# Reordering the gate/up matmuls of one contraction step in an expert-choice encoder block

## The chip, the cores and the metric

The kernel runs on one core of one Trainium2 chip. The metric is the device time of one execution in microseconds (us), taken as the median of several runs. A profile of one more execution gives the time of each instruction.

## The reference, cut to what matters

One encoder block is applied to a prompt of 1024 tokens and a sample of 512 tokens with shared weights: attention and Fourier mixing, a gated output projection, then a mixture of 16 experts, then a norm. All data are fp32. The change is inside the experts. An expert takes its 192 best tokens (128 of the prompt, 64 of the sample) of width 1024 and runs a gated two-layer network of inner width 2048 on them:

```python
def expert_choice(xn, w_router, w_eg, w_eu, w_ed):
    ...
    aff = jax.nn.softmax((xt @ w_router).astype(jnp.float32), axis=-1)
    gate, idx = lax.top_k(aff.T, C)
    xe = xt[idx]
    h = jax.nn.silu(jnp.einsum('ecd,edf->ecf', xe, w_eg)) * jnp.einsum('ecd,edf->ecf', xe, w_eu)
    ye = jnp.einsum('ecf,efd->ecd', h, w_ed) * gate[..., None].astype(xn.dtype)
    out = jnp.zeros((T, D), xn.dtype).at[idx.reshape(-1)].add(ye.reshape(-1, D))
```

## The kernel before, in words

Each fp32 operand of a large product is split into a high part (rounded to fp32r) and a low part (the rest, also fp32r), and a product is made of three: high by high, high by low and low by high. For the experts the weights are split into `wh` (ScalarE, L1477) and `wl` (VectorE, L1520), and the 192 gathered tokens into `xsplit`, where the high columns and the low columns of one contraction step `k` lie side by side, 2 x 192 = 384 columns (CAP is 192).

The program of each engine is written out by hand, and engines wait for each other through counters (semaphores). TensorE runs its instructions in the written order. Its program for the experts is a loop over 16 experts; each does `gate_up` and then `down`.

`gate_up` loops over 16 blocks `q` of 128 inner columns. A block makes two outputs, `part` 0 (gate) and `part` 1 (up), each in its own PSUM bank, `2 * (q % 2) + part`. For each part it runs through 8 contraction steps `k`. One step has two matmuls, each with a weight tile of its own of 128 x 128:

- L1432: `wh` tile, 384 moving columns, into columns 0 to 383 of the bank (high and low tokens).
- L1434: `wl` tile, 192 moving columns (high tokens), added onto columns 192 to 383 of the same bank.

So a block has 2 x 8 x 2 = 32 matmuls and as many weight loads. Before its first matmul TensorE waits until the block's weights are cut (`w_cut`) and until the sums of the block two earlier, which used the same banks, have been taken out (`gu_sum`). After the block's last matmul one counter, `w_used`, is raised. ScalarE waits for it, copies the low columns of both banks out (L1491), splits a later weight block (L1477), and takes the sigmoid (L1498); VectorE adds the two halves of both banks (L1536), cuts the low weights (L1520) and forms the product of gate and up (L1543, L1545).

`down` multiplies the split inner activations `hsplit` with the down weights in matmuls of 512 columns, five per contraction step (L1451 to L1456), and `turn_tokens` transposes the next expert's tokens in its midst (L1416, L1417). The SyncE queue loads the raw weights (L1125), and it waits on `w_cut`, not on TensorE's order inside a block.

Other products of TensorE that the prediction compares with are the input projection (L549 to L551, 256 columns, fp32r) and the router's logits (L1175, 16 columns).

Of the kernel before, what the change touches and what calls it, by code (L numbers as in the profile page):

```python
# [34 lines left out]
P = 128  # L35
D = 1024
KT = D // P
# [118 lines left out]
def encoder(nc, x, rel_bias, norm1_g, w_in, w_attn_br, w_four_br, w_gate, b_gate, w_out, norm2_g,  # L156
            w_router, w_eg, w_eu, w_ed, final_g, identity, one_hot, pos_prompt, pos_sample, chan, y):
    ctx = ExitStack()
    with ctx:
# [161 lines left out]
        with nc.Block() as block:  # L321
            @block.sync
            def _(sp):
                sp.dma_start(relb[0:BUCKETS, :], rel_bias).then_inc(h_loaded, 16)
                sp.dma_start(hot[:, :], one_hot).then_inc(h_loaded, 16)
                for s in range(4):
                    sp.dma_start(xin[:, s, :], x[s * P:(s + 1) * P, :]).then_inc(x_in_ld[s], 16)
                    if s == 0:
                        sp.dma_start(g1[:, :], norm1_g.partition_broadcast(P)).then_inc(c_loaded, 16)
                        sp.dma_start(ident[:, :], identity).then_inc(c_loaded, 16)  # L330
                sp.dma_start(bg[:, :], b_gate).then_inc(c_loaded, 16)
                sp.dma_start(wr[:, :, :], w_router[0].rearrange("(k p) e -> p k e", p=P)).then_inc(c_loaded, 16)
                for n in range(2):
                    load_in_block(sp, n)
                with sp.Fori(1, NT // 4) as i:
                    for s in range(4):
                        sp.wait_ge(n_xs, i * 4 + (s - 3))
                        sp.dma_start(xin[:, s, :], x[bass.ds(i * 4 * P + s * P, P), :]).then_inc(x_in_ld[s], 16)

                sp.wait_ge(t_sb, ROWS_T // 2)  # L340
                sp.wait_ge(t_sbD, ROWS_T // 2)
                sp.dma_start(toep, toep_sb[:, :, :]).then_inc(t_out, 16)
# [1016 lines left out]
        with nc.Block() as block:  # L1359
# [48 lines left out]
            @block.tensor  # L1408
            def _(pe):
                def turn_tokens(n):  # L1410

                    pe.wait_ge(x_in, (n + 1) * 32)
                    pe.wait_ge(gu_sum, n * FT + GU_PAIRS)
                    for k in range(KT):
                        at_col = (k % 2) * CAP
                        pe.transpose(ps[:, k // 2, at_col:at_col + CAPS[0]], xg[0][:, k * P:(k + 1) * P], ident[:, :])  # L1416
                        mm = pe.transpose(ps[:, k // 2, at_col + CAPS[0]:at_col + CAP], xg[1][:, k * P:(k + 1) * P],  # L1417
                                          ident[0:CAPS[1], 0:CAPS[1]])
                        if k % 4 == 3:
                            mm.then_inc(x_T, 1)  # L1420

                def gate_up(e):
                    pe.wait_ge(x_cut, (e + 1) * 2)
                    for q in range(FT):
                        pe.wait_ge(w_cut, e * SUBS + (q + 1))
                        pe.wait_ge(gu_sum, e * FT + (q + 1))
                        for part in range(2):
                            bank = 2 * (q % 2) + part
                            for k in range(KT):
                                tile = slice((8 * part + k) * P, (8 * part + k + 1) * P)  # L1430

                                pe.matmul(ps[:, bank, 0:2 * CAP], wh[:, q % AHEAD, tile],  # L1432
                                          xsplit[:, k, :, :].rearrange("p s t -> p (s t)"), start=k == 0, stop=False)
                                mm = pe.matmul(ps[:, bank, CAP:2 * CAP], wl[:, q % AHEAD, tile], xsplit[:, k, 0, :],  # L1434
                                               start=False, stop=k == KT - 1)
                        mm.then_inc(w_used, 1)

                def down(e, last):
                    for i in range(8):
                        q, c = FT + i, i // 4  # L1440
                        pe.wait_ge(w_cut, e * SUBS + (q + 1))
                        if i < 4:
                            pe.wait_ge(h_cut, e * 8 + 2 * (i + 1))
                        if i % 4 == 0:
                            pe.wait_ge(y_ev, e * 2 + (c + 1))
                        for kk in range(4):
                            k = 4 * (i % 4) + kk
                            cols = slice(kk * CH, (kk + 1) * CH)
                            first, end = k == 0, k == FT - 1
                            prompt, sample = ps[:, 4 + 2 * c, :], ps[:, 5 + 2 * c, :]  # L1450
                            pe.matmul(prompt, hsplit[:, k, H_LOW], wh[:, q % AHEAD, cols], start=first, stop=False)  # L1451
                            pe.matmul(prompt, hsplit[:, k, H_HIGH], wh[:, q % AHEAD, cols], start=False, stop=False)  # L1452
                            pe.matmul(prompt, hsplit[:, k, H_HIGH], wl[:, q % AHEAD, cols], start=False, stop=end)  # L1453

                            pe.matmul(sample, hsplit[:, k, H_SAMPLE], wh[:, q % AHEAD, cols], start=first, stop=False)  # L1455
                            mm = pe.matmul(sample, hsplit[:, k, H_SAMPLE], wl[:, q % AHEAD, cols], start=False, stop=end)  # L1456
                        mm.then_inc(w_used, 1)
                        if i == 1 and not last:
                            turn_tokens(e + 1)

                turn_tokens(0)
                with pe.Fori(0, E - 1) as e:
                    gate_up(e)
                    down(e, False)
                gate_up(E - 1)
                down(E - 1, True)

# [183 lines left out]
```

## Time and profile before

| what | value |
|---|---|
| median of 3 runs | 3463.94 us (3463.56 to 3468.08) |
| span of the profiled execution, first to last instruction | 3481.5 us |
| TensorE matmul busy | 3295.9 us, 95% of the span |
| TensorE weight load busy | 2868.7 us, 82% |
| VectorE busy | 1858.5 us, 53% |
| ScalarE busy | 1433.8 us, 41% |
| DMA | 543.03 MB, mean 156 GB/s |

The span is all that the profile gives of the profiled execution's own time; it is 17.6 us (0.5%) above the median of the runs without it. A matmul is recorded as two instructions: a weight load (PEld in the rows) and the matmul itself (PE). The matmuls overlap in their records, so a matmul's recorded duration is longer than the time it adds; what it adds is read from the distance of starts.

### The profile page before, as it was taken

Reading aid. Unit: us, or ns where it says so; the run is one execution under the profiler, and the core shown is the slowest. Engines: PE = TensorE matmul, PEld = TensorE weight load, DVE = VectorE, ACT = ScalarE, POOL = GpSimd, SP = SyncE. Lnnn points to the kernel's source line nnn. Section 1 sums busy time; section 2 is a strip of 40 time slices with the busy share of each in tenths; the row PEclk is TensorE's granted clock in tenths of the full one; section 3 lists DMA queues with packets and bytes.
Section 4 is the critical chain, followed back from the end, with each engine's and each line's share of the span. In section 5 each row is a group of like instructions: output and inputs, shape, how many; then the busy total and the mean of one; then the engine's idle time right before and its main releaser. Section 6 shows DMA issues by size and latency. Waiting matters only on the chain. (4 is left out here: it accounts for less than half of the span.)

```text
span 3481.5 us, 45734 instructions
## 1 busy us (share of the span) xinstructions
PE 3295.9 (95%) x17656; PEld 2868.7 (82%) x17656; DVE 1858.5 (53%) x2770; ACT 1433.8 (41%) x1969; POOL 122.3 (4%) x133
## 2 busy tenths in 40 slices
PE   6999999999999999985999999999999999999994
PEld 4978989896487786544999999999999999999993
DVE  4140221305334332276677777777776777777774
ACT  4030120312333321323555555655565555555553
POOL 0000000000000000000000000000000000000000
PEclk9969979699999999986999999999999999999997
DMA  4000000003132335223677767777677767776774
GB/s 161 25 32 25 14 18 25 31 13 109 44 98 87 95 121 175 91 79 130 227 235 239 241 220 245 235 239 231 238 244 234 241 229 237 234 242 222 246 227 160
DMA packets 456895, 543.03 MB, mean 156 GB/s; under 512 B 13131, under 2 KB 372811, under 8 KB 456684
## 3 DMA queue, kind: packets, MB, share of 16 engines
q1 hardware_dynamic: 449644, 516.71, 44.1%
q0 software_dynamic: 7168, 25.17, 3.2%
q8 instruction: 57, 0.93, 0.1%
q14 instruction: 26, 0.21, 0.0%
HBM read 502.37 MB, written 39.47 MB: 156 GB/s over the span
## 5 line engine op out<-in xcount | busy, mean ns | idle before, releaser
L1432 PE MATMUL ps<-xsplit,wh 128*128 128x384 f32 x4096 | 1168.9, 360 | 2.2 <-DVE xsplit L1527 2.2
L1434 PE MATMUL ps<-xsplit,wl 128*128 128x192 f32 x4096 | 1026.6, 251 | 0.0
L1520 DVE TENSOR_TENSOR wl<-raw,wh 128x2048 fp32r<-128x2048 f32 x384 | 876.7, 2283 | 116.4 <-ACT wh L1477 115.3
L1477 ACT ACTIVATE wh<-raw 128x2048 fp32r<-128x2048 f32 x384 | 734.1, 1912 | 349.1 <-PE ps L1456 323.2
L1434 PEld LDWEIGHTS ps<-xsplit,wl 128*128 128x128 f32 x4096 | 784.0, 191 | 0.6
L1432 PEld LDWEIGHTS ps<-xsplit,wh 128*128 128x128 f32 x4096 | 770.2, 188 | 3.0 <-issue 2.4
L1491 ACT ACTIVATE low<-ps 128x384 f32<-128x384 f32 x256 | 126.0, 492 | 435.4 <-PE ps L1434 435.4
L1536 DVE TENSOR_TENSOR gu<-ps,low 128x384 f32<-128x384 f32 x256 | 142.8, 558 | 221.1 <-ACT low L1491 220.0
L1049 DVE TENSOR_TENSOR glow<-graw,ghigh 128x1024 fp32r<-128x1024 f32 x72 | 88.1, 1225 | 235.7 <-ACT ghigh L1005 235.7
L549 PE MATMUL ps<-whigh,xhigh 128*128 128x256 f32 x624 | 203.7, 326 | 3.5 <-ACT u L683 2.8
L550 PE MATMUL ps<-wlow,xhigh 128*128 128x256 f32 x624 | 203.6, 326 | 0.0
L551 PE MATMUL ps<-whigh,xlow 128*128 128x256 f32 x624 | 203.5, 326 | 0.0
L1451 PE MATMUL ps<-wh,hsplit 128*128 128x512 f32 x512 | 202.5, 395 | 0.0
L1453 PE MATMUL ps<-wl,hsplit 128*128 128x512 f32 x512 | 200.6, 392 | 0.0
L1455 PE MATMUL ps<-wh,hsplit 128*128 128x512 f32 x512 | 200.6, 392 | 0.0
L1456 PE MATMUL ps<-wl,hsplit 128*128 128x512 f32 x512 | 200.4, 391 | 0.0
L1452 PE MATMUL ps<-wh,hsplit 128*128 128x512 f32 x512 | 200.4, 391 | 0.0
L654 ACT ACTIVATE sc<-sc,negm 128x128 f32<-128x128 f32 (+2 forms) x144 | 61.9, 430 | 278.2 <-DVE negm L702 278.1
L1005 ACT ACTIVATE ghigh<-graw 128x1024 fp32r<-128x1024 f32 x72 | 76.3, 1060 | 213.9 <-DMA graw<-in_w_gate_dram 138.4
L990 PE MATMUL ps<-xh,ghigh 128*128 128x512 f32 x384 | 151.8, 395 | 13.1 <-DVE xlow L1056 13.1
L549 PEld LDWEIGHTS ps<-whigh,xhigh 128*128 128x128 f32 x624 | 153.6, 246 | 3.9 <-ACT u L683 3.0
L550 PEld LDWEIGHTS ps<-wlow,xhigh 128*128 128x128 f32 x624 | 153.6, 246 | 0.0
(205 smaller groups left out, 4626.7 us busy)
## 6 DMA issues: line engine op xcount, KB each, us to landing
raw<-in_w_exp_gate_dram SPq DMA_DIRECT2D x128, 1024.0 KB, 5.6
raw<-in_w_exp_up_dram SPq DMA_DIRECT2D x128, 1024.0 KB, 7.8
raw<-in_w_exp_down_dram SPq DMA_DIRECT2D x128, 1024.0 KB, 6.9
graw<-in_w_gate_dram SPq DMA_DIRECT2D x96, 256.0 KB, 2.9
wraw<-in_w_in_dram SPq DMA_DIRECT2D x12, 1024.0 KB, 5.0
graw<-in_w_four_br_dram SPq DMA_DIRECT2D x24, 384.0 KB, 3.5
xin<-in_x_dram SPq DMA_DIRECT2D x12, 512.0 KB, 3.9
xres<-in_x_dram SPq DMA_DIRECT2D x12, 512.0 KB, 3.6
```

The source lines that it names most:

```text
L549: pe.matmul(bank, high[k], whigh[:, n % 2, k, :], start=k == 0, stop=False)
L550: pe.matmul(bank, high[k], wlow[:, n % 2, k, :], start=False, stop=False)
L551: mm = pe.matmul(bank, low[k], whigh[:, n % 2, k, :], start=False, stop=k == KT - 1)
L1432: pe.matmul(ps[:, bank, 0:2 * CAP], wh[:, q % AHEAD, tile], xsplit[:, k, :, :].rearrange("p s t -> p (s t)"), start=k == 0, stop=False)
L1434: mm = pe.matmul(ps[:, bank, CAP:2 * CAP], wl[:, q % AHEAD, tile], xsplit[:, k, 0, :], start=False, stop=k == KT - 1)
L1451: pe.matmul(prompt, hsplit[:, k, H_LOW], wh[:, q % AHEAD, cols], start=first, stop=False)
L1452: pe.matmul(prompt, hsplit[:, k, H_HIGH], wh[:, q % AHEAD, cols], start=False, stop=False)
L1453: pe.matmul(prompt, hsplit[:, k, H_HIGH], wl[:, q % AHEAD, cols], start=False, stop=end)
L1455: pe.matmul(sample, hsplit[:, k, H_SAMPLE], wh[:, q % AHEAD, cols], start=first, stop=False)
L1456: mm = pe.matmul(sample, hsplit[:, k, H_SAMPLE], wl[:, q % AHEAD, cols], start=False, stop=end)
L1477: act.activation(cut_part(wh, q), raw_part(q), ACT.Copy).then_inc(w_high, 1)
L1520: dve.tensor_tensor(cut_part(wl, q), raw_part(q), cut_part(wh, q).bitcast(F32), ALU.subtract).then_inc(w_cut, 1)
```

## The change

Inside a block the loops over part and contraction step are exchanged, and within a step the two 384-column matmuls (gate, up) come first and then the two 192-column ones (gate, up). The number of matmuls, their operands, their banks, the order of the additions into each bank, the waits and the one counter raised at the block's end are the same.

```diff
                         pe.wait_ge(w_cut, e * SUBS + (q + 1))
                         pe.wait_ge(gu_sum, e * FT + (q + 1))
-                        for part in range(2):
-                            bank = 2 * (q % 2) + part
-                            for k in range(KT):
-                                tile = slice((8 * part + k) * P, (8 * part + k + 1) * P)
-
+                        for k in range(KT):
+                            gate_up_tiles = [(2 * (q % 2) + part, slice((8 * part + k) * P, (8 * part + k + 1) * P)) for part in range(2)]
+                            for bank, tile in gate_up_tiles:
                                 pe.matmul(ps[:, bank, 0:2 * CAP], wh[:, q % AHEAD, tile],
                                           xsplit[:, k, :, :].rearrange("p s t -> p (s t)"), start=k == 0, stop=False)
+                            for bank, tile in gate_up_tiles:
                                 mm = pe.matmul(ps[:, bank, CAP:2 * CAP], wl[:, q % AHEAD, tile], xsplit[:, k, 0, :],
                                                start=False, stop=k == KT - 1)
                         mm.then_inc(w_used, 1)
```

## Rows read from the trace of the kernel before

**Rows 1.** The profile's page: the span, and each engine's busy time.
```profile
span 3481.5 us, 45734 instructions
...
PE 3295.9 (95%) x17656; PEld 2868.7 (82%) x17656; DVE 1858.5 (53%) x2770; ACT 1433.8 (41%) x1969; POOL 122.3 (4%) x133
```

**Rows 2.** The page's costliest groups: the two gate/up matmuls (count, busy, mean).
```profile
L1432 PE MATMUL ps<-xsplit,wh 128*128 128x384 f32 x4096 | 1168.9, 360 | 2.2 <-DVE xsplit L1527 2.2
L1434 PE MATMUL ps<-xsplit,wl 128*128 128x192 f32 x4096 | 1026.6, 251 | 0.0
```

**Rows 3.** Busy time by stretch: one expert's `gate_up`, columns as its first line says.
```profile
core 0: us, PE busy (x) PEld busy (x) DVE busy (x) ACT busy (x) POOL busy (x), PEclk, DMA share, GB/s
2075.10:2148.00 72.90, 72.90 (x514) 72.86 (x513) 56.30 (x77) 46.15 (x56) 7.95 (x8) 1.00 0.72 239
```

**Rows 4.** TensorE's waits over the expert stage, 1619 to 3440 us, all of them.
```profile
PE ps L1432 <- DVE xsplit L1527: 2.2, 1, 2.2
```

**Rows 5.** Timeline, start of that `gate_up`: start us, us, engine, line.
```profile
2074.91 0.39 PE L1456 MATMUL ps<-wl,hsplit 128*128 128x512 f32 x1
2074.91 0.19 PEld L1432 LDWEIGHTS ps<-xsplit,wh 128*128 128x128 f32 x1
2075.13 0.33 PE L1432 MATMUL ps<-xsplit,wh 128*128 128x384 f32 x1
2075.14 0.19 PEld L1434 LDWEIGHTS ps<-xsplit,wl 128*128 128x128 f32 x1
2075.30 0.25 PE L1434 MATMUL ps<-xsplit,wl 128*128 128x192 f32 x1
2075.31 0.19 PEld L1432 LDWEIGHTS ps<-xsplit,wh 128*128 128x128 f32 x1
...
2075.39 0.36 PE L1432 MATMUL ps<-xsplit,wh 128*128 128x384 f32 x1
2075.41 0.19 PEld L1434 LDWEIGHTS ps<-xsplit,wl 128*128 128x128 f32 x1
```

**Rows 6.** Groups by line within 2075 to 2188 us: the expert's long gate/up matmuls.
```profile
L1432 PE MATMUL ps<-xsplit,wh 128*128 128x384 f32 x256 | 72.9, 359 | 0.0
```

**Rows 7.** Timeline, end of that `gate_up`: its last matmul and the next.
```profile
2147.84 0.25 PE L1434 MATMUL ps<-xsplit,wl 128*128 128x192 f32 x1
2147.92 0.41 PE L1451 MATMUL ps<-wh,hsplit 128*128 128x512 f32 x1
```

**Rows 8.** Timeline, the reading of one block's banks by ScalarE and VectorE.
```profile
2007.92 0.49 ACT L1491 ACTIVATE low<-ps 128x384 f32<-128x384 f32 x1 [1.60 <-PE ps L1434]
...
2008.44 0.56 DVE L1536 TENSOR_TENSOR gu<-ps,low 128x384 f32<-128x384 f32 x1 [0.60 <-ACT low L1491]
```

**Rows 9.** Timeline, input projection, 256 columns: first and last of 314 matmuls.
```profile
683.41 0.28 PE L550 MATMUL ps<-wlow,xhigh 128*128 128x256 f32 x1
...
720.97 0.28 PE L551 MATMUL ps<-whigh,xlow 128*128 128x256 f32 x1
```

**Rows 10.** Timeline, down product, 512 columns: first, three inner, last of 25.
```profile
2038.49 0.39 PE L1451 MATMUL ps<-wh,hsplit 128*128 128x512 f32 x1
...
2041.21 0.39 PE L1453 MATMUL ps<-wl,hsplit 128*128 128x512 f32 x1
2041.44 0.39 PE L1455 MATMUL ps<-wh,hsplit 128*128 128x512 f32 x1
2041.66 0.39 PE L1456 MATMUL ps<-wl,hsplit 128*128 128x512 f32 x1
...
2043.93 0.39 PE L1456 MATMUL ps<-wl,hsplit 128*128 128x512 f32 x1
```

**Rows 11.** Timeline, router's logits, 16 columns: sixteen weight loads in one row.
```profile
1549.75 1.87 PEld L1175 LDWEIGHTS ps<-wr,xn2T 128*128 128x128 f32 x16
```

**Rows 12.** Timeline, weight loads of the token transposes inside `down`.
```profile
2044.82 0.14 PEld L1417 LDWEIGHTS ps<-ident,xgS 64*128 64x128 f32 x1
2045.03 0.14 PEld L1416 LDWEIGHTS ps<-ident,xgP 128*128 128x128 f32 x1
2045.29 0.13 PEld L1417 LDWEIGHTS ps<-ident,xgS 64*128 64x128 f32 x1
```

## The prediction

> **What bounds the kernel now.** I read the page first: TensorE is busy for 95% of the span, the next engine for 53% [rows 1]. The two gate/up matmuls, 4096 of each, are its costliest groups [rows 2]. They lie in 16 experts; in the `gate_up` of one, 72.9 us long, TensorE is busy for all 72.90 us at a granted clock of 1.00, the higher of its two levels, while VectorE has 56.30 and ScalarE 46.15 [rows 3]. In the whole expert stage TensorE waits for another engine once, for 2.2 us [rows 4]. So the stage lasts as long as TensorE's own stream of loads and matmuls, and anything that this stream gains or loses is gained or lost by the kernel: 16 x 72.9 = 1166 us are at stake.
>
> **The cadence before.** The first short matmul of that expert starts at 2075.30 [rows 5], the last at 2147.84 [rows 7]; there are 256 [rows 6], thus 255 pairs in 72.54 us, 284.5 ns for a pair of one long (384) and one short (192) matmul. What makes up this number decides the prediction.
>
> Streaming first. The 512-column matmuls come 24 intervals in 5.44 us, 226.7 ns apart [rows 10]; the 256-column ones 313 intervals in 37.56 us, 120.0 ns [rows 9]. That is 0.417 ns a column and 13.3 ns a matmul. By this line a long one would take 173.3 ns and a short one 93.3, together 266.6. The pair takes 17.9 ns more, 73 us over 4096 pairs, and the question is whether the new order gives any of that back.
>
> The weight loads say where it goes. A load starts with the start of the matmul ahead of it, not earlier: 2075.14 after the matmul at 2075.13, 2075.31 after 2075.30 [rows 5]. So one tile can wait while another is in use, and no more. Under a long matmul the load is done in time: a long one begun after a 512-column one has its short successor start 0.17 us later (2075.13 to 2075.30). Under a short one it isn't: the load begun at 2075.31 is followed by the next one only at 2075.41, 0.10 us later, although the 192 columns are through before that. The 16-column matmuls show the same limit alone: 16 loads in 1.87 us, and with 0.19 for the record of the last, as of the loads in [rows 5], 15 intervals of 112 ns [rows 11], whatever the matmul. With 173 for the long one and 112 for the short one the pair comes to 285, and 284.5 is measured. So a long matmul costs its streaming, a short one costs the load of whatever comes next, and neither lends the other its slack.
>
> **The change, part by part.** It removes and adds no instruction: a step of one `k` has two long and two short matmuls and four loads in both orders, and there are 16 x 16 x 8 = 2048 steps. No DMA is issued in the moved lines, and no wait stands between them. What changes is the neighbours:
>
> - Two long ones in a row: the second is a long matmul that begins with its weights ready. Its price is between the 0.17 us of [rows 5] and the 173.3 ns of the line; call it 172.
> - Long to short stays as it is.
> - Two short ones in a row: the second starts when its load is done, like a long one now, and then the next load begins. This case, one load-bound start after another, doesn't occur in the present gate/up. The nearest row is the 16-column chain with the same 128 x 128 tile, 112 ns. From below the smallest distance is a load's own pace, 0.10 to 0.11 us in [rows 5], say 107. From above it is 120: a 256-column matmul has a load of fp32r weights under it too and needs no longer [rows 9]. I take 112, the row nearest in kind, since nothing but loads binds there.
>
> Of the four intervals of a step, one long and one short keep the sum of today's pair, 284.5. The other two are the second long one and the second short one: 172 + 112 = 284 in place of 284.5. The difference is -0.5 ns x 2048 = -1 us. With the ends: (170 + 107 - 284.5) x 2048 = -15 us, and (173.3 + 120 - 284.5) x 2048 = +18 us.
>
> The Trainium skill, page "TensorE: Matmul & The Clock Gate", section "LDWEIGHTS (loading the stationary operand)", gives a weight load as its columns divided by 1.2 in ns, which is 106.7 for 128. The second short interval at that price would make the step 172 + 106.7 - 284.5 = -5.8 ns and the kernel 12 us faster, an estimate; the 16-column chain's 112 ns [rows 11] stands against it, so I leave it as the lower case. The same page, in "Step-by-step: what each phase is for", says that loads are pulled ahead of running matmuls within a 64-deep window. Were that more than one tile ahead, the pairs of today would run at the streaming sum of 266.6; they take 284.5.
>
> Edits costed at nothing: the gate bank is now complete only at the block's end instead of its middle. Nobody notices, because the one counter was raised at the end before as well: ScalarE reads both banks from 2007.92 for 0.49 us and VectorE adds them from 2008.44 for 0.56, done at 2009.00 [rows 8]. These banks are needed again one block after, 16 pairs or 4.55 us later, so some 3.5 us of cover remain; without it TensorE would wait about 1.1 us in each of 256 blocks, 280 us. The first matmul of a block carries the same two waits, so the weights' loads and cuts see the same dates.
>
> **The sum.** The profiled span is 3481.5 us [rows 1], 17.6 us above the median of the runs, and gives its intervals only as differences; -1 us put onto the median of 3463.9 gives 3463 us.
>
> **The rivals.**
>
> - *Turn-free loads*, faster: the second of two load-bound starts costs a bare load, 107 ns, and the second long one 170 to 172. Then the step is 5.5 to 7.5 ns shorter, 11 to 15 us: 3449 to 3453. For it speaks the 0.10 between two loads in [rows 5]; against it the 112 of [rows 11].
> - *The bank*, faster: today each short matmul adds onto columns that the long one just wrote in the same bank, and the 17.9 ns above the streaming sum are a wait for that. The new order puts another bank's matmul between, and the whole 73 us come back: 3391. Against it: in the 512-column chain the bank changes between L1453 and L1455 and not between L1455 and L1456, and the distances are 0.23 and 0.22 [rows 10]; and the loads explain the excess without it.
> - *The full turn*, slower: the second short one pays a matmul's 13.3 ns on top of the load, 120 ns. The step becomes 172 + 120 - 284.5 = 7.5 ns longer, 15 us, with 173.3 for the long one 18: 3479 to 3482. It decides from 115.9 ns on (284.5 - 172 + 3.4, as 3.4 x 2048 = 7 us). For it: all fp32r rows that stream carry these 13.3 ns; against it, 173 + 120 would have made today's pair 293. Farther out lie the transposes, whose loads come 0.21 and 0.26 us apart [rows 12]; 235 in place of 112 would cost 250 us, but they alternate tiles of 64 and 128 rows, which no gate/up tile does.
> - *Order without effect* is the forecast itself: four matmuls cost what they cost whatever their neighbours.
>
> **How the numbers follow.** A measurement of this kernel tells from no change what is above 0.2%, 6.9 us. I give the forecast 0.74, its own range 3457 to 3470; turn-free loads 0.10; the bank 0.03; the full turn 0.10, and something larger on that side, as in [rows 12], 0.03. So faster 0.13, same 0.74, slower 0.13. The range from 3451 to 3482 holds the forecast, the full turn and most of the turn-free case, and leaves out the bank and the large loss.
>
> **What would show it right or wrong.** One expert's `gate_up` should last 72.8 us again, with TensorE busy throughout. In it the starts after a matmul should read about 0.20 (long to long, as today's matmul that waits for its load is recorded early), 0.17 (long to short), 0.09 (short to short) and 0.11 (short to long), in sum 0.57. The loads should be 0.11 apart twice and 0.17 twice. A long-to-long or long-to-short distance near 0.17 together with short ones at 0.09 throughout would show the bank; a sum of 0.58 the full turn. TensorE waits other than the one of 2.2 us would mean that an engine behind it has become late. The prediction fails if a load can start before the matmul ahead of it does, or if two short matmuls of different banks are dearer than two loads.

## The result and the profile after

The changed kernel takes 3481.53 us (median of 4 runs, 3479.60 to 3482.79), the kernel before 3464.02 us: a ratio of 1.0046, 95% interval 1.0032 to 1.0060, so it is slower by about 16 us by that ratio and by 17.5 by the two medians. No change was forecast, and the time lies just inside the stated range, at its far end.

The page of the changed kernel, its span, TensorE's busy time and the two groups that answer to [rows 2]:

```profile
span 3479.3 us, 45734 instructions
...
PE 3293.9 (95%) x17656; PEld 2866.0 (82%) x17656; DVE 1857.2 (53%) x2770; ACT 1433.8 (41%) x1969; POOL 119.7 (3%) x133
...
L1430 PE MATMUL ps<-xsplit,wh 128*128 128x384 f32 x4096 | 1100.5, 350 | 2.2 <-DVE xsplit L1526 2.2
...
L1433 PE MATMUL ps<-xsplit,wl 128*128 128x192 f32 x4096 | 741.0, 262 | 0.0
```

Two things on this page mislead. The busy sums of the two groups fall by 68 and 286 us against [rows 2], because matmuls of one line now overlap each other in their records; the kernel isn't faster for it. And the span is 2.2 us shorter than that of [rows 1]: in that earlier execution the first expert's first gate/up matmul started only at 1619.0 us, here at 1603.2, because the clock was low for longer in the stages ahead (276 us against 236), which neither order of the gate/up matmuls touches. Over the twelve traces of this document that start moves by 0.4 us for each us at the lower clock ahead of it. The experts have to be compared with each other.

The start and the end of one expert's `gate_up`, as in [rows 5] and [rows 7] (matmuls of one line that follow each other are one row, the last column their count):

```profile
2061.67 0.39 PE L1455 MATMUL ps<-wl,hsplit 128*128 128x512 f32 x1
2061.90 0.51 PE L1430 MATMUL ps<-xsplit,wh 128*128 128x384 f32 x2
2062.25 0.36 PE L1433 MATMUL ps<-xsplit,wl 128*128 128x192 f32 x2
2062.45 0.53 PE L1430 MATMUL ps<-xsplit,wh 128*128 128x384 f32 x2
...
2135.06 0.36 PE L1433 MATMUL ps<-xsplit,wl 128*128 128x192 f32 x2
2135.26 0.42 PE L1450 MATMUL ps<-wh,hsplit 128*128 128x512 f32 x1
```

From the first long matmul to the first matmul of `down` it takes 73.36 us here, and 2147.92 - 2075.13 = 72.79 in [rows 5, 7]. The same is seen from expert to expert. The first long matmul of the next expert here, and of the expert before that of [rows 5] in the kernel before:

```profile
2175.35 0.33 PE L1430 MATMUL ps<-xsplit,wh 128*128 128x384 f32 x1
...
1962.23 0.33 PE L1432 MATMUL ps<-xsplit,wh 128*128 128x384 f32 x1
```

2175.35 - 2061.90 = 113.45 us in place of 2075.13 - 1962.23 = 112.90, and these two numbers come again wherever the clock doesn't fall, so 16 x 0.55 = 8.8 us. That is half of the loss.

The other half is the clock. The busy time by stretch around the token transposes of two experts of the changed kernel (the columns are those of [rows 3], the last but two the granted clock), and last of one expert of the kernel before:

```profile
2029.30:2033.00 3.70, 3.70 (x18) 2.10 (x16) 1.65 (x3) 2.67 (x3) 0.00 (x0) 1.00 1.08 382
2033.30:2036.60 3.30, 3.30 (x9) 2.61 (x8) 2.65 (x3) 0.61 (x2) 0.00 (x0) 0.50 0.26 92
...
2144.40:2148.10 3.70, 3.70 (x18) 2.13 (x16) 1.65 (x3) 2.67 (x3) 0.00 (x0) 1.00 1.08 381
2148.40:2151.70 3.30, 3.30 (x16) 2.73 (x15) 2.68 (x3) 0.59 (x2) 0.00 (x0) 1.00 0.25 88
...
2157.00:2160.70 3.70, 3.70 (x18) 2.05 (x16) 1.65 (x3) 2.67 (x3) 0.00 (x0) 1.00 1.08 382
2161.30:2164.60 3.30, 3.30 (x9) 2.63 (x8) 2.90 (x3) 0.37 (x1) 0.00 (x0) 0.50 0.18 63
```

In all three, TensorE runs the 16 transposes for 3.7 us at the higher level. Behind the first and the last stretch the clock falls to half, to the lower level, and 9 matmuls lie in the next 3.3 us instead of 16; behind the second one it doesn't. An expert with such a fall is 1.6 us longer (115.06 us to the next one). There are 15 such stretches in the expert stage, one for each expert that has a next one. The trace of the changed kernel has 7 falls there, behind every second or third stretch, that of before 3 (from 1707.3, 2161.2 and 2953.1 us on), and another trace with the distance of before has 2 (e1 below). With the 8.8 us of cadence, 4 to 5 more falls at 1.6 us make 15 to 17.

### The profile page after: what moved, and what is told of

Read it like the earlier page. It is cut to its first block and busy times, and to the rows that moved or that the text cites. A ratio compares the mean times of both kernels' runs of the same rounds, so it can differ in the third digit from the quotient of the medians.

```text
span 3479.3 us, 45734 instructions
## 1 busy us (share of the span) xinstructions
PE 3293.9 (95%) x17656; PEld 2866.0 (82%) x17656; DVE 1857.2 (53%) x2770; ACT 1433.8 (41%) x1969; POOL 119.7 (3%) x133
## 5 line engine op out<-in xcount | busy, mean ns | idle before, releaser
L1430 PE MATMUL ps<-xsplit,wh 128*128 128x384 f32 x4096 | 1100.5, 350 | 2.2 <-DVE xsplit L1526 2.2
L1433 PEld LDWEIGHTS ps<-xsplit,wl 128*128 128x128 f32 x4096 | 742.0, 188 | 0.0
L1433 PE MATMUL ps<-xsplit,wl 128*128 128x192 f32 x4096 | 741.0, 262 | 0.0
L1430 PEld LDWEIGHTS ps<-xsplit,wh 128*128 128x128 f32 x4096 | 622.1, 192 | 3.5 <-issue 2.4
```

What stands on the lines that cost most here:

```text
L1430: pe.matmul(ps[:, bank, 0:2 * CAP], wh[:, q % AHEAD, tile], xsplit[:, k, :, :].rearrange("p s t -> p (s t)"), start=k == 0, stop=False)
```

## The experiments

Each comparison below was run against the kernel before on the same chip. "Distance" is the time from one expert's first gate/up matmul to the next one's where the clock doesn't fall, read from the trace, and "falls" are the stretches of lower clock in the expert stage of the one profiled execution. All of them begin within 0.9 us of the start of an expert's last transpose.

| kernel | distance, us | falls | ratio to before (95%) |
|---|---|---|---|
| before | 112.90 | 3 | |
| changed | 113.45 | 7 | 1.0046 (1.0032 to 1.0060) |
| e1: loops exchanged, alternating | 112.90 | 2 | 0.9999 (0.9990 to 1.0009) |
| e2: groups of 2 in one bank | 113.45 | 7 | 1.0042 (1.0030 to 1.0054) |
| e3: groups of 16 | 113.25 | 5 | 1.0027 (1.0018 to 1.0037) |
| e9: groups of 4 | 113.87 | 10 | 1.0079 (1.0067 to 1.0092) |
| e4: before, 64 more matmuls | 122.02 | 8 | one run, 3620.2 us |
| e5: before, 3 more long matmuls | 113.41 | 5 | 1.0037 (1.0025 to 1.0050) |
| e6: changed, 16 more long matmuls | 116.25 | 3 | 1.0149 (1.0126 to 1.0171) |
| e7: before, transposes spread | 113.37 | 0 | 1.0011 (1.0002 to 1.0021) |
| e8: changed, transposes spread | 113.92 | 0 | 1.0035 (1.0023 to 1.0046) |
| e10: before, transposes in halves | 112.99 | 0 | 0.9989 (0.9980 to 0.9999) |

**One part alone: the loops (e1).**

```diff
+for k in range(KT):
+    for part in range(2):
+        bank, tile = 2 * (q % 2) + part, slice((8 * part + k) * P, (8 * part + k + 1) * P)
         pe.matmul(ps[:, bank, 0:2 * CAP], wh[...], ...)
         mm = pe.matmul(ps[:, bank, CAP:2 * CAP], wl[...], ...)
```

> The loops over part and k are exchanged as in the change, but long and short matmuls still alternate (gate long, gate short, up long, up short). Theory of the loads (what costs is a short matmul right behind a short one): nothing changes, 568.8 ns for four matmuls, 72.70 us for the gate_up of one expert, 112.90 us from expert to expert, 3464 us. Rival (the banks: what costs is that gate and up alternate within a step): 573 ns for four matmuls, 73.24 us for one gate_up as in the changed kernel, 3473 us or more.

Measured: the distance is that of before, 112.90, and the time is too. Exchanging the loops, and with them alternating the banks from pair to pair, costs nothing.

**The other part alone: the groups (e2).** Here long and short stand for the two matmul calls:

```diff
 for part in range(2):
     bank = 2 * (q % 2) + part
-    for k in range(KT):
-        long(k); short(k)
+    for pair in range(0, KT, 2):
+        long(pair); long(pair + 1); short(pair); short(pair + 1)
```

> The loops stay as before (one part, one bank at a time), but two contraction steps are grouped: long, long, short, short, all into one bank. Theory of the loads: the cadence of the changed kernel, 573 ns for four matmuls and 73.24 us for the gate_up of one expert, 3473 us by the cadence alone and about 3481 us if the granted clock falls as often as in the changed kernel. Rival (the banks): 72.70 us and 3464 us.

Measured: the changed kernel's numbers, with the loops and banks of before. Its `gate_up`, again from the first long matmul to the first of `down`:

```profile
2062.04 0.51 PE L1432 MATMUL ps<-xsplit,wh 128*128 128x384 f32 x2
...
2135.39 0.42 PE L1452 MATMUL ps<-wh,hsplit 128*128 128x512 f32 x1
```

73.35 us, as 73.36 in the changed kernel. With e1 this settles the first question: what costs is that two long and two short matmuls stand together, and not where they write.

**The prices by themselves (e4).** Sixty-four matmuls, whose results the first block overwrites, run ahead of each expert:

```diff
+if q == 0:
+    def probe(i, n, bank):
+        cols = xsplit[:, i % KT, :, :].rearrange("p s t -> p (s t)")[:, 0:n]
+        pe.matmul(ps[:, bank, 0:n], wh[:, 0, i % 16 * P:(i % 16 + 1) * P], cols, start=True, stop=True)
+    for i in range(16):
+        probe(i, 384, 0)
+    for i in range(16):
+        probe(i, 384, i % 2)
+    for i in range(16):
+        probe(i, 192, 0)
+    for i in range(16):
+        probe(i, 192, i % 2)
```

> Before the first block of each expert 64 more matmuls run whose results the first block overwrites: 16 long into one bank, 16 long into two banks by turns, 16 short into one bank, 16 short into two by turns, each with a weight tile of its own. Theory of the loads: 173 ns from long to long, 112 to 115 ns from short to short, no difference between one bank and two, about 9.2 us more for each expert and 3611 us in all. Rival (the banks): chains in one bank and in two differ by some 5 ns or more. Rival (the full turn): 120 ns from short to short.

One run, 3620.2 us. The timeline, in order: long ones into one bank, into two by turns (matmuls), short ones into one bank, into two (their loads):

```profile
2097.90 1.37 PE L1430 MATMUL ps<-xsplit,wh 128*128 128x384 f32 x7
...
2099.46 2.76 PE L1430 MATMUL ps<-xsplit,wh 128*128 128x384 f32 x15
...
2102.40 1.31 PEld L1430 LDWEIGHTS ps<-xsplit,wh 128*128 128x128 f32 x11
...
2104.07 1.42 PEld L1430 LDWEIGHTS ps<-xsplit,wh 128*128 128x128 f32 x12
```

A row's length less the record of its last instruction (0.33 and 0.19), divided by the intervals: 173 and 174 ns from long to long, 112 and 112 from short to short. Both prices are what the prediction worked with, one bank or two. The rival of the full turn (120 ns) falls. A change of bank has no price here; the probes add onto nothing, so they don't test a wait for sums just written. But the chain showed something else: the long ones follow the 512-column matmuls of the expert before, and the first distances between them, the same in each expert (medians of the starts in the trace), are 171, 175, 177, 185, 176 and 182 ns before they settle at 173. A long matmul's price depends on its place in the run. This trace also has 8 falls of the clock, at 122.02 us from expert to expert.

**Longer groups (e3, e9).** All 16 long matmuls of a block first, and then all 16 short ones; and the same in groups of four (the diff is that of e9, where long and short stand for the two matmul calls; e3 takes all 16 at once):

```diff
+all_tiles = [(k, bank of part, tile of part and k) for k in range(KT) for part in range(2)]
+for four in range(0, 2 * KT, 4):
+    for k, bank, tile in all_tiles[four:four + 4]: long
+    for k, bank, tile in all_tiles[four:four + 4]: short
```

> The suspected cost is doubled: within a block all 16 long matmuls come first, then all 16 short ones. Theory of the loads, charged to each short matmul that follows a short one (15 per block in place of 8, 4.5 ns each): 73.8 us for one gate_up, 3481 us by the cadence, and more where the granted clock falls more often. Rival (charged to each change from long to short or back, 1 per block in place of 8): 72.8 us for one gate_up and 3465 us.

Measured for e3: 0.35 us more per expert than before, less than with groups of two (0.55), and neither theory's number: a charge for each short one behind a short one would have given about 1.1, a charge for each passage 0.1. Both fall. The trace shows where it sits. The loads around the passage from short to long, those of 16 short matmuls, of the first two long ones behind the run, and of the next five (a load starts with the matmul ahead of it):

```profile
2001.07 1.93 PEld L1432 LDWEIGHTS ps<-xsplit,wl 128*128 128x128 f32 x16
...
2002.91 0.30 PEld L1429 LDWEIGHTS ps<-xsplit,wh 128*128 128x128 f32 x2
...
2003.21 0.89 PEld L1429 LDWEIGHTS ps<-xsplit,wh 128*128 128x128 f32 x5
```

The short ones' loads are 112 ns apart, as in the chain. From the second long one's load on, the starts in the trace are 180, 176, 182 and then 173 ns apart (medians), where the settled price is 173: a run of short ones is paid for by the first three long ones behind it. From this came a number for groups of four, which have four such passages in a block, and in each group only the fourth long matmul has settled:

> Groups of four: four long matmuls (two contraction steps, gate and up), then four short ones. Theory of the settling (the first three long matmuls behind a run of short ones take about 180, 176 and 181 ns and only later ones 173, a short one 112 and the first of a run 108): 1154 ns for eight matmuls against 1137 when they alternate, 73.74 us for the gate_up of one expert, more than with groups of two (73.24) and of sixteen (73.05). Rival (a fixed charge of 4.5 ns for each change from short to long beyond the alternation): 73.0 us.

Measured for e9: 0.97 us more per expert than before, the worst of all groups, with the predicted settling in its loads (medians 180, 176, 182, 173, then 108, 111, 112 and 112). Its `gate_up`:

```profile
2076.86 0.51 PE L1430 MATMUL ps<-xsplit,wh 128*128 128x384 f32 x2
...
2150.63 0.42 PE L1450 MATMUL ps<-wh,hsplit 128*128 128x512 f32 x1
```

73.77 us against 72.79 before. A cost that rises from groups of two to four and falls again to sixteen is what the settling says and what a fixed charge for a passage doesn't.

**The clock without the groups (e5).** The order of before, with three long matmuls more per expert:

```diff
+if q == 0:
+    for i in range(3):
+        pe.matmul(ps[:, 0, 0:2 * CAP], wh[:, 0, i % 16 * P:(i % 16 + 1) * P],
+                  xsplit[:, i % KT, :, :].rearrange("p s t -> p (s t)"), start=True, stop=True)
```

> The kernel before, in its own order, with three more long matmuls at the start of each expert whose results are overwritten: about 0.52 us more for each expert, so that experts follow each other at 113.42 us, as in the changed kernel (113.45), without any grouping. Theory of the distance (how often the granted clock falls behind the token transposes depends on the distance from expert to expert, not on the order of the matmuls): 7 falls in the expert stage in place of 2 or 3, 1.6 us each, and 8.3 us of cadence, in all some 16 us above the kernel before. Rival (the grouped matmuls themselves draw the falls): 2 or 3 falls, 8 us above the kernel before.

Measured: a ratio of 1.0037, 13 us, of which 16 x 0.51 = 8 us are the added matmuls; 5 falls in the profiled execution, which was the fastest of six (3472.3 us; the median is 3479.4 at a lower mean clock). None of its gate/up matmuls is grouped, and it still loses some 5 us more than it was given to do. That speaks for the distance, though one profile with 5 falls against an expected 7 leaves the count rough.

**The clock with the groups, at another distance (e6).** The same insertion, sixteen times, in the changed kernel:

> The changed kernel with sixteen more long matmuls at the start of each expert whose results are overwritten: 2.77 us more for each expert, 44 us in all, experts 116.23 us apart. Theory of the distance (the number of falls follows the distance from expert to expert, and not in proportion to it): clearly fewer falls than the 7 of the changed kernel, 2 or 3, and 3518 us. Rival (the falls belong to the grouped matmuls): 7 falls, 3526 us.

Measured: 3518.5 us (two runs), and 3 falls instead of 7. With the groups in place the falls grow rare at this distance. It isn't that more distance means fewer falls: e4, with the gate/up order of before, has 8 at 122.02 us. So the count goes by the distance, not in proportion to it, and not by the grouped matmuls.

**The clock without the stretch of transposes (e7, e8).** In both kernels a pair of transposes behind each five 512-column matmuls, over two blocks of the down product:

```diff
 mm = pe.matmul(sample, hsplit[:, k, H_SAMPLE], wl[...], ...)
+if i in (1, 2) and not last and (i, kk) != (1, 0):
+    turn_tokens(e + 1, [4 * (i - 1) + kk - 1])
...
-if i == 1 and not last:
-    turn_tokens(e + 1)
+if i == 2 and not last:
+    turn_tokens(e + 1, [KT - 1])
```

> The kernel before, with the eight pairs of token transposes no longer in one stretch inside the down product but one pair behind each five 512-column matmuls. Theory of the transposes (the clock falls because of the stretch of 3.7 us that holds only transposes): no fall is left in the expert stage, 3 to 5 us less; and if the loads of the transposes hide under the long matmuls, up to 2 us less for each expert, 30 us more. Rival (the falls have another cause): as many falls as before, and no gain or a loss from the mixing.

> The changed kernel, with the token transposes spread in the same way. Theory of two parts (half of the change's loss is cadence, half is falls of the clock behind the transposes): no fall is left, and the kernel is 8.6 us slower than the kernel before with spread transposes, not 16. Rival (one cause): still 16 us slower than that.

Measured: no fall is left in either. The distance alone doesn't explain that: e7 lies as far from expert to expert as e5 (113.37 and 113.41), e8 as far as e9 (113.92 and 113.87), and those have 5 and 10 falls. So the falls go with the unbroken stretch of transposes. The distance grows by 0.47 us, so the hoped-for gain from hiding the transposes' loads didn't come; each mixing of transposes and long matmuls costs some. For e7 that is 15 x 0.47 = 7.1 us lost against 2 or 3 falls, some 4 us, gained, and its median is 3.6 us above that of before. Without falls the two orders are 0.55 us an expert apart (113.92 and 113.37), 8.8 us, and their medians 3476.9 - 3469.5 = 7.4 us. So the two halves of the loss are separate: this is the cadence alone, and the rest of the 16 us went with the falls.

**A version without the falls (e10).** The order of before, with the transposes in two stretches of four pairs:

```diff
-if i == 1 and not last:
-    turn_tokens(e + 1)
+if i in (1, 2) and not last:
+    turn_tokens(e + 1, range(4 * (i - 1), 4 * i))
```

> The kernel before, with the token transposes in two stretches of four pairs, behind the second and the third block of the down product, in place of one stretch of eight. If the falls need the long stretch: no fall in the expert stage, one more passage between transposes and long matmuls for each expert (0.06 us, an eighth of the 0.46 us that seven more of them cost when the pairs were spread), 2 to 4 us less than the kernel before. Rival (half a stretch is enough for a fall): as many falls as before or more, no gain.

Measured: no fall, 0.09 us more per expert, 3463.4 us against 3465.9, a ratio of 0.9989 (0.9980 to 0.9999), an interval that ends just below 1. It is the fastest of all, by a tenth of a per cent. It was run at one distance only, so that half a stretch draws no fall at any other isn't shown. The busy time by stretch over most of the expert stage, columns as in [rows 3], here and in the kernel before (its two falls in this window vanish in the rounding of the clock):

```profile
1720.00:3300.00 1580.00, 1580.00 (x9625) 1466.83 (x9624) 1146.55 (x1372) 904.89 (x1008) 107.83 (x112) 1.00 0.72 236
...
1720.00:3300.00 1580.00, 1580.00 (x9617) 1468.52 (x9616) 1147.60 (x1372) 904.89 (x1008) 108.95 (x112) 1.00 0.72 236
```

In the changed kernel fewer matmuls fit into the same 1580 us, at a mean clock of 0.99:

```profile
1720.00:3300.00 1580.00, 1580.00 (x9544) 1468.69 (x9543) 1138.31 (x1365) 896.74 (x1004) 106.29 (x112) 0.99 0.71 234
```

**The two terms together.** Sixteen times what the distance grew (fifteen times where the transposes make it grow), and 1.6 us for each fall above the 2 or 3 of before, taken as 2.5, meet the differences of the medians within 2 us in every kernel of the table: 16.0 and 17.5 for the changed kernel, 9.6 and 8.5 for e3, 27.5 and 28.6 for e9, 12.2 and 13.5 for e5, -2.6 and -2.5 for e10.

## Why the prediction was wrong

**What bounds the kernel** was read rightly: TensorE waits once in the changed expert stage too, for 2.2 us, and every change of its cadence went straight into the time. The edits costed at nothing cost nothing: e1 has the gate bank finished late as well.

**The step that failed** is "Of the four intervals of a step, one long and one short keep the sum of today's pair, 284.5." The other two terms were nearly right: the second short one was put at 112 and takes 111, the second long one was put at 172 and takes 174. But the pair doesn't keep its sum: the first long one and the first short one take 180 + 108 = 288. The loads of the changed kernel, and after them the numbers of the trace:

```profile
2062.64 0.36 PEld L1433 LDWEIGHTS ps<-xsplit,wl 128*128 128x128 f32 x2
2062.93 0.30 PEld L1430 LDWEIGHTS ps<-xsplit,wh 128*128 128x128 f32 x2
2063.22 0.36 PEld L1433 LDWEIGHTS ps<-xsplit,wl 128*128 128x128 f32 x2
```

From one step to the next 0.58 us by these rows, and over the 2048 steps the median distances of the loads are 174, 108, 111 and 180 ns, 573 in all; in the kernel before they are 108 and 176, twice, 569. So the first long matmul behind two short ones takes 180, not the 176 that it takes behind one, and the second long one 2 ns more than was put down: 4.5 ns a step, 9 us over 2048, where the working had -0.5 ns and its far end +8.8. The prediction treated a price as belonging to a matmul and its neighbour; it belongs to the run. The check of these prices against the pair of before was luck: 173 + 112 = 285 met the measured 284.5, but that pair is 176 + 108, and the two errors cancel.

**The second step that failed** was not a number but a reading. The cadence of one expert at a clock of 1.00 [rows 3] stood for the stage, and the rare falls behind the transposes, which the trace of before has too, got no term in the sum. They aren't common to both kernels: how often the clock falls depends on the distance from expert to expert, and a change of 0.5% in it took them from 2 or 3 to 7, 1.6 us each. That about doubled the loss. Neither of the two ways to fail that the prediction named happened: no load starts before the matmul ahead of it, and two short matmuls aren't dearer than two loads (111). And that the time lies inside the range is luck, since its upper end stood for the full turn.

**The rivals.** The full turn had the right time, 3479 to 3482, for a wrong reason: two short matmuls in a row are 112 ns apart and not 120 (e4), and the coincidence comes from the falls. The bank is excluded by the changed kernel, which puts another bank's matmul between and isn't faster, and by e2, which stays in one bank and takes the same time as the changed kernel. Turn-free loads are excluded by the 111 of the second short one and the 112 of the chain. The Trainium skill, page "TensorE: Matmul & The Clock Gate", section "LDWEIGHTS (loading the stationary operand)", gives a load its columns divided by 1.2 in ns, an estimate of 106.7 for 128 columns; the chain's 112 from load to load is the price here.

**The signs named beforehand** were too coarse: 0.20, 0.17, 0.09 and 0.11 were forecast for the four distances and were found (200, 175, 88 and 111 ns), with a sum of 0.57 as forecast. A step of 573 and one of 569 read nearly the same in rows of 10 ns; the length of a whole `gate_up`, forecast at 72.8 and found at 73.36, told them apart.

**What stays open.** Why a long matmul needs up to six of its kind to settle, at 175 to 185 ns, isn't shown. A wait for the weights alone is unlikely, since in e4 it comes behind 512-column matmuls, which start 227 ns apart, twice the 112 of a load; no run tests it. Why one distance draws more falls than another isn't shown either, and the falls were counted in one execution of each kernel.

## What to carry to other kernels

When an engine is the bound, a reordering of equal work is priced by the length of a whole stretch, not by prices of single instructions added up: passages between matmuls of different lengths cost several ns for a few matmuls. Here a steady alternation was best, and runs of sixteen lost less than groups of two or four. And before a loop's length is changed by a little, look for a rare loss inside it (here a stretch of transposes that the clock sometimes answers) whose frequency depends on that length. Breaking that stretch in two won 2.5 us here, while every grouping of the gate/up matmuls lost.

## What the runs showed of the hardware that was not expected

- Long matmuls (384 columns, fp32r, each with its own tile) settle at 173 ns from start to start only after some six of them behind 512-column ones (171, 175, 177, 185, 176, 182), and after three behind a run of short ones (180, 176, 182).
- Strict alternation of long and short (284.4 ns a pair) is slightly cheaper than the settled prices of both (173.3 + 111.7 = 285.0).
- Behind the same 3.7 us of transposes at the higher clock level the clock fell to the lower one in 2 or 3 of 15 experts at a distance of 112.90 us, in 5 at 113.25 and at 113.41, in 7 at 113.45, in 10 at 113.87, in 3 at 116.25 and in 8 at 122.02, and in none at 112.99 where the transposes came in two stretches of half the length.
- Sixteen transposes mixed one pair at a time into 512-column matmuls cost 0.47 us more per expert than in one stretch.
